# Attention stage of a hybrid encoder: who makes the normalised rows before the router

## The reference, cut to what matters

```
h = rms_norm(x, norm_mix_g);  p = h @ w_in            # conv part and q, k, v
o = stick_breaking_attention(q, k, v)                 # 8 heads of 64
x = x + concat(conv_out, attn_out) @ w_out
h2 = rms_norm(x, norm_ffn_g)                          # x * rsqrt(mean(x*x)+eps) * g
x = x + hierarchical_moe(h2, ...)                     # router: h2 @ w_rg, h2 @ w_re
```

## Time and profile before

| | us | share of the span |
|---|---|---|
| median of three runs | 2204.78 | |
| the profiled execution, its own time | 2202.57 | |
| its span, first to last instruction | 2200.8 | |
| TensorE busy | 2088.1 | 95% |
| VectorE busy | 1623.4 | 74% |
| ScalarE busy | 1260.0 | 57% |
| GpSimd busy | 806.9 | 37% |

### The profile page before, as it was taken

One profiled execution on the slowest core, in us unless ns is written; L12 is line 12 of the kernel. 1 busy time (PEld: TensorE's weight loads), 2 busy tenths in 40 slices (PEclk: granted clock), 3 DMA queues, 4 the chain that ended last, 5 costly groups with the idle time before them and its releaser, 6 DMA issues. The chain is left out here.

```text
span 2200.8 us, 40164 instructions
## 1 busy us (share of the span) xinstructions
PE 2088.1 (95%) x13505; PEld 1771.5 (80%) x13506; DVE 1623.4 (74%) x2083; ACT 1260.0 (57%) x2200; POOL 806.9 (37%) x689
## 2 busy tenths in 40 slices
PE   8999999995899999899999895999999999999998
PEld 6888888884687887678787774888888888888887
DVE  3799999984777667867878967969698556556644
ACT  5322433335677777866676643768588555456533
POOL 1111544553566654545545435222222222222221
PEclk9999999996999999999999996999999999999999
DMA  7553344334333242333222117989899968767852
GB/s 228 186 191 134 118 128 159 120 106 144 114 117 109 80 131 81 108 105 116 80 73 92 54 70 258 361 281 372 308 357 373 329 197 282 228 198 264 285 172 35
DMA packets 211517, 393.17 MB, mean 179 GB/s; under 512 B 54749, under 2 KB 81757, under 8 KB 211389
## 3 DMA queue, kind: packets, MB, share of 16 engines
q1 hardware_dynamic: 197853, 357.42, 47.1%
q0 software_dynamic: 13536, 34.12, 6.8%
HBM read 315.42 MB, written 91.23 MB: 185 GB/s over the span
## 5 line engine op out<-in xcount | busy, mean ns | idle before, releaser
L2428 DVE TENSOR_TENSOR p_w_lo<-p_raw,p_w_hi 128x1024 fp32r<-128x1024 f32 (+1 forms) x260 | 439.5, 1728 | 150.5 <-ACT p_w_hi L2223 149.9
L2051 POOL TENSOR_TENSOR p_wgt<-p_wgt,p_past 128x1024 f32<-128x1024 f32 (+4 forms) x166 | 308.5, 1859 | 347.2 <-DVE p_past L1929 347.1
L2223 ACT ACTIVATE p_w_hi<-p_raw 128x2048 fp32r<-128x2048 f32 (+1 forms) x198 | 361.8, 1859 | 84.0 <-PE p_up L2310 67.3
L762 DVE SCALAR_TENSOR_TENSOR p_ut<-p_ut,p_cw 128x512 f32<-128x512 f32 (+1 forms) x480 | 329.2, 762 | 0.0
L1929 DVE TENSOR_TENSOR_SCAN p_past<-p_keep,p_past,p_one 128x513 f32<-128x513 f32 (+1 forms) x196 | 225.9, 1193 | 75.3 <-ACT p_keep L1746 73.3
L1746 ACT ACTIVATE p_keep<-p_zp 128x512 f32<-128x512 f32 (+3 forms) x326 | 158.8, 547 | 119.2 <-PE p_zp L1620 106.5
L2310 PE MATMUL p_gp<-p_w_hi,p_xt_hi 128*128 128x256 f32 x736 | 210.4, 286 | 0.0
L436 PE MATMUL p_pj<-p_w_hi,p_xt_hi 128*128 128x512 f32 x512 | 205.2, 401 | 4.2 <-DVE p_xt_lo L738 2.4
L2310 PE MATMUL p_gp<-p_w_lo,p_xt_hi 128*128 128x256 f32 x736 | 206.5, 281 | 0.0
L2310 PE MATMUL p_gp<-p_w_hi,p_xt_lo 128*128 128x256 f32 x736 | 206.4, 280 | 0.0
L436 PE MATMUL p_pj<-p_w_hi,p_xt_lo 128*128 128x512 f32 x512 | 200.6, 392 | 0.0
(11 more groups left out here) (309 smaller groups left out, 4975.6 us busy)
## 6 DMA issues: line engine op xcount, KB each, us to landing
p_raw<-in_w_up SPq DMA_DIRECT2D x128, 512.0 KB
p_raw<-in_w_gate SPq DMA_DIRECT2D x128, 512.0 KB
p_raw<-in_w_down SPq DMA_DIRECT2D x128, 512.0 KB
wide_raw<-in_w_in SPq DMA_DIRECT2D x56, 256.0 KB, 3.8
wide_raw<-in_x SPq DMA_DIRECT2D x17, 512.0 KB
scr_y<-wide_raw SPq DMA_DIRECT2D x17, 512.0 KB, 3.1
wide_raw<-scr_y SPq DMA_DIRECT2D x17, 512.0 KB
y_out<-wide_raw SPq DMA_DIRECT2D x17, 512.0 KB, 2.9
```

What stands on the lines that cost most here:

```text
L762: dve.scalar_tensor_tensor(dst, src, cw[:, a, j:j + 1], dst, ALU.mult, ALU.add).then_inc(tap_done, 1)
L2051: pool.tensor_tensor(mine, mine, past_rows[:, u % NP, 0:n, 2:2 + w], ALU.mult).then_inc(a_done, 1)
L2223: act.activation(part(w_hi, p, wide), raw[:, n % RING:n % RING + wide, :], ACT.Copy).then_inc(whi_done, wide)
L2428: dve.tensor_tensor(part(w_lo, p, wide), raw[:, n % RING:n % RING + wide, :], part(w_hi, p, wide).bitcast(F32), ALU.subtract).then_inc(wlo ...
```

## The change

For the 15 tiles `by_pool` (m = 17 to 31), GpSimd multiplies x by the norm's weights into h2, in two halves of 128x512, in step `end_step`+2 behind the product of that step (`gained`). ScalarE then multiplies h2 in place by the inverse root of its row (`scaled`): the first half in step `end_step`+3, the second in +4, behind the sigmoids of that step and ahead of the first job and the copies. Each `scaled` waits until both halves of `gained` of its tile are done. VectorE's `hidden` stays for the last two tiles only. The costs in `by_act` follow: 6 on ScalarE's side in place of 10 on VectorE's; with them nine second-half copies go from ScalarE to VectorE, those of steps 112, 124, 130, 131, 147, 151, 158, 165 and 166.

```diff
@@ -1263,7 +1263,7 @@
                                                   sem("o_done"))
         m_hi_done, m_done, y_done = sem("m_hi_done"), sem("m_done"), sem("y_done")
         st_y, st_o, st_h = ring("st_y", 3), ring("st_o", 4), ring("st_h", 2)
-        ss_done, rs_step, h2_done = sem("ss_done"), sem("rs_step"), sem("h2_done")
+        ss_done, rs_step, h2_done, yg_done = sem("ss_done"), sem("rs_step"), sem("h2_done"), sem("yg_done")
         h2t_done, lg_done = sem("h2t_done"), sem("lg_done")
         picked, chosen_done, ranked, rank_consts = sem("picked"), sem("chosen_done"), sem("ranked"), sem("rank_consts")
 
@@ -1315,6 +1315,7 @@
         pick_step = {b: where["route", NT + hi - 1] for b, (lo, hi) in enumerate(BATCHES)}
         hidden_step = [{m: e + (3 + c if e < end else 1 if m < 2 * NT - 1 else 2)
                         for m, e in end_step.items() if m >= NT} for c in range(2)]
+        by_pool = [m for m in end_step if NT <= m < 2 * NT - 2 and end_step[m] < end]
         square_step = {m: e + 1 if e < end else e for m, e in end_step.items() if m >= NT}
         y_step = {m: where["wo", m, 0] - AHEAD for m in range(2 * NT)}
         for m in range(3, 2 * NT):
@@ -1329,7 +1330,8 @@
             act = 5 * w + 6 + sum(act_cost.get(j[0], 0) for j in jobs[s]) + 4 * (s in o_step_of)
             dve = 7 * w + sum(dve_cost.get(j[0], 0) for j in jobs[s]) + 4 * (s - 1 in o_step_of)
             act += 10 * sum(1 for m, e in end_step.items() if m >= NT and e == s - 1)
-            dve += 10 * sum(1 for half in hidden_step for e in half.values() if e == s)
+            act += 6 * sum(1 for half in hidden_step for m, e in half.items() if e == s and m in by_pool)
+            dve += 10 * sum(1 for half in hidden_step for m, e in half.items() if e == s and m not in by_pool)
             dve += 30 * sum(1 for e in pick_step.values() if e in (s - 1, s - 2))
             by_act += [True, act < dve][0:half_count(units[u])]
         act_copies = [0]
@@ -1783,6 +1785,12 @@
                     act.wait_ge(mp_full, use["h2t", m - 2, 1] + 1)
                 act.activation(h2[:, r % 2, :], y[:, m % 3, :], ACT.Square, accum_out=ss).then_inc(ss_done, 1)
 
+            def scaled(m, c):
+                r, mine = m - NT, slice(c * C, (c + 1) * C)
+                act.wait_ge(yg_done, 2 * by_pool.index(m) + 2)
+                act.wait_ge(rs_step, 2 * r + 2)
+                act.activation(h2[:, r % 2, mine], h2[:, r % 2, mine], ACT.Copy, scale=rstd).then_inc(h2_done, 1)
+
             for j in jobs[-1]:
                 job(j)
             for s in range(steps):
@@ -1792,6 +1800,10 @@
                     split(m)
                 if s < len(units):
                     sigmoids(s)
+                for c in (1, 0):
+                    for m in at_step(hidden_step[c], s):
+                        if m in by_pool:
+                            scaled(m, c)
                 for j in ahead(s):
                     job(j)
                 if 0 <= s - 3 < len(units):
@@ -1959,7 +1971,8 @@
             for s in range(steps):
                 for c in (1, 0) if s < len(units) else (0, 1):
                     for m in at_step(hidden_step[c], s):
-                        hidden(m, c)
+                        if m not in by_pool:
+                            hidden(m, c)
                 if s < len(units):
                     scan(s)
                 elif s - 1 in o_step_of:
@@ -2042,6 +2055,14 @@
                 pool.wait_ge(rs_step, 2 * r + 1)
                 pool.tensor_tensor(rstd, rt, mhalf[:, 0:1], ALU.pow).then_inc(rs_step, 1)
 
+            def gained(m):
+                r = m - NT
+                pool.wait_ge(const_in, 48)
+                for c in range(2):
+                    mine = slice(c * C, (c + 1) * C)
+                    pool.tensor_tensor(h2[:, r % 2, mine], y[:, m % 3, mine], g2[:, mine],
+                                       ALU.mult).then_inc(yg_done, 1)
+
             def product(u):
                 w = width(u)
                 n = half_count(units[u])
@@ -2062,6 +2083,9 @@
                         inverse_rms(m)
                 if s < len(units):
                     product(s)
+                for m in at_step(end_step, s - 2):
+                    if m in by_pool:
+                        gained(m)
     return sems
 
 
```

## The result

The changed kernel takes 2214.55 us (median of six, 2212.92 to 2219.8) against 2204.05 for the kernel before (2202.55 to 2205.7): 10.5 us slower by the medians. The ratio is 1.0054, 95% interval 1.0044 to 1.0064, which is 11.9 us (9.7 to 14.1). I had predicted 2206 with 2197 to 2213. The profiled execution has a span of 2212.1 us against 2200.8.

The account below looks back on a forecast made before the run. TensorE was taken to bound the 15-tile stage, busy 331.4 of 350 us. Profiled 2202.57 - 11.3 + 12.8 = 2204.1, plus 2.2 to the median, 2206.3; predicted 2206 us, range 2197 to 2213.

Parts of the forecast that it names:

- What the change removes: VectorE's 30 gain instructions in the 15-tile stage: 9.6 us of TensorE idle time removed, 11.3 with the clock.
- the idle time of 2.35 us at 1231: TensorE idle behind VectorE's gain instructions: worth all 2.35 us, and the clock's 1.7 behind it.
- the other four: TensorE idle times ended by VectorE: gains 0.75 us at 1072, 1.79 at 1085, 1.50 at 1163.5, 3.24 at 1260.6.
- What it adds on GpSimd: Thirty products of 128x512 at 1.19 us, 2.38 per tile, 36 us in all, lengthening nothing by themselves.
- What it adds on ScalarE: Thirty scalings at 0.70 us, 21 us fitting its idle time; nine moved copies between -1 and +1 us; the price is the wait.
- the prediction's chain: Per tile: GpSimd product's end + 2.38 + 0.70 scaling + 0.60 first copy, against the start of TensorE's transposition.
- The waits in steps 124, 157 and 165: TensorE waits for ScalarE's copy behind `scaled`: 3.0, 2.5 and 4.7 us, the last paid in full.
- Sum 10.2 us of new idle time: TensorE's new waits in steps 124, 157 and 165, plus 2.6 us for half of three clock losses: 12.8 us.
- My own sign of being wrong: TensorE's idle time from 940 to 1300 changing over 4 us, scans beyond 1.3 us, or stages before and after differing.
- Rival 1: Waits on `gained` reach TensorE only in step 165; faster, 2197.4 us; chance 0.28.
- Rival 2: Copies behind `scaled`: ScalarE held behind GpSimd reaches TensorE at most tiles once multiplications take 1.5 us; 2212.3 us; chance 0.29.
- Rival 3: Contention: GpSimd's 36 us of multiplications hold VectorE's scans as long; 2216.2 us; chance 0.03.

Follow-up runs that it names:

- e13: Kernel before, VectorE's 30 gain instructions made sums over 8 columns, not waiting for GpSimd's inverse root, nothing added; attention stage 335.4 us against 343.8.
- e8: Kernel before, plus 30 GpSimd multiplications of 128x512 to a spare place, nobody waiting for them; ratio to before 1.0020.
- e3: Kernel before, plus 30 ScalarE scalings of 128x512 to a spare place, waiting for no other engine; ratio to before 1.0005.
- e6: Changed kernel with the planner's old costs, so the nine second-half copies stay on ScalarE; ratio to before 1.0059.
- e12: Kernel before, VectorE's 30 gain instructions reading 8 columns of one SBUF operand, nothing added; attention stage 339.8 us against 343.8.
- e9: Kernel before, VectorE's 30 gain instructions making 8 columns in place of 512, nothing added; attention stage 339.6 us against 343.8.

## Why the prediction was wrong, by its own steps

- "What the change removes", 9.6 us of idle time and 1.7 of clock: too high. The relief by itself is 8.4 us (e13), 6.2 of them idle time. I counted the idle time of 2.35 us at 1231 as "worth all"; the same run of picking ended a later wait, 1.71 us in the change and in e13 alike. Of the other four, those at 1085 and 1260 went, at 1072 1.60 us were left (1.75 forecast; 1.96 in e13), and at 1163 1.94 in e13 (1.60 forecast); in the change that one lies behind the new idle time.
- "What it adds on GpSimd", 1.19 us: it is 1.28, the other row. That it lengthens nothing by itself was wrong: alone it cost 4.4 us in e8, in part by holding the picking. The prediction had named the picking as the one thing held, and put no price on it.
- "What it adds on ScalarE", scalings and copies at nothing: right as far as the intervals of e3 and e6 reach. Behind a late wait the scaling costs, as the prediction's chain had it.
- The waits in steps 124, 157 and 165, forecast 3.0, 2.5 and 4.7 us: 2.96, 2.01 and 4.68 us. Right, with the mechanism.
- **The step that failed** is the line under them: "Sum 10.2 us of new idle time; half of three clock losses is 2.6; together 12.8." First, I tested each tile against the first copy behind `scaled` only. In step 138 that copy had 0.7 us to spare (1148.05 + 2.19 + 3.68 = 1153.9 against a transposition at 1154.66), but behind it stood the second copy and the `h2t` eviction: 1148.05 + 2.19 + 2.38 + 0.70 + 1.01 for both copies + 0.75 = 1155.1 against the `wo` product at 1151.80. That is 3.3 us, and 3.31 were measured. Second, the clock: I took one fall of 1.7 us per idle time and half of them. All four long idle times had a fall in them or behind them, two of them of 3.4 us, and one fall came without a long idle time.
- In the sum's terms: TensorE's idle time should have grown by 0.6 us (10.2 - 9.6) and grew by 5.8, 3.3 of it in step 138. The clock's loss should have grown by 0.9 (2.6 - 1.7) and grew by 7.5 in the profiled pair, by about 5 over all executions. My own sign of being wrong, a change of more than 4 us in TensorE's idle time, was met; scans beyond 1.3 us were not.
- Rival 1 (only step 165 waits) fell. Rival 2 was near in time (2212.3). Late evictions, `h2t` among them, were its too, but it wanted multiplications of 1.5 us or more for them, and they took 1.28; one eviction and the clock did it. Rival 3 in its form (scans held) fell: 25 scans of 128x513 that ran for nine tenths of their time or more beside a GpSimd product or multiplication in the change took 1.26 to 1.28 us, the other 147 took 1.19 to 1.28. The Trainium skill's rule in "SBUF — State Buffer", section "Who interferes with whom", held for the picking and not for the scan. The same section counts `tensor_scalar` among the operations that can enter the two-port modes, in which one SBUF input is enough to contend, and the e12 row (2.07 us for 8 columns) agrees.

What stays open: how the falls of the clock are placed. In the fifteen traces, 29 of 38 idle times of 2 us or more in this stretch had a fall in them or within 2 us behind them, and 9 had none. A fall near 1190 follows an idle time of only 0.73 us in the change and in seven of the experiments, and not in the kernel before. The execution of e3 had five falls and a stage of 348.6 us, with TensorE's idle time in it as before (18.1 us) and a median hardly above that of before. So a single trace can't tell what the clock costs to better than some 5 us.

## What to carry to other kernels

When work is moved to an engine that feeds the bottleneck, look at what stands behind it in that engine's queue before looking at its busy time: 30 scalings by themselves cost nothing that could be measured, and one wait ahead of the copies cost about 9 us. Test the delay against every instruction behind the wait, evictions too, and treat the last place before a stage's end as paid in full (here one tile of fifteen made 7 of the 11.9 us). If TensorE is busy 95% of the time, price each idle time over 2 us with the fall of the clock that tends to come with it (29 of 38 here, 1.7 or 3.4 us each), and put a moved producer ahead of, and its consumer behind, the work that others wait for.

## What the runs showed of the hardware that I had not expected

- A fall of the clock can last twice as long as those of the trace before: 3.4 us lost in one piece around 1080 to 1092 and 1294 to 1304 us, behind an idle time of 2.96 us and from within one of 4.68 us.
- A VectorE instruction of 8 columns took 2.06 us beside GpSimd's product, with two operands from SBUF (e9, where the shortest of its kind took 0.20 us) and with one and a scalar (e12), while a sum over 8 columns (e13) took 0.13 to 0.16 us, also the 16 of 30 that ran beside a GpSimd instruction of over 1 us. In the mean of 29:

```profile
L1956 DVE TENSOR_REDUCE p_h<-wide_raw 128x1 f32<-128x8 f32 x29 | 4.3, 150 | 0.1
```
